# Recurrent mixer: the triangular solve's products cut to 32x32 blocks, and the solve's place in a slot made to alternate

## The reference, cut to what matters

```python
def wkv_scan(s0, scan_in):
    def step(s, inp):
        w, kk, a, k, v, r = inp
        sa = jnp.einsum('dbhij,dbhj->dbhi', s, kk)
        s = s * w[..., None, :] - sa[..., :, None] * (kk * a)[..., None, :] + v[..., :, None] * k[..., None, :]
        return s, jnp.einsum('dbhij,dbhj->dbhi', s, r)
    return lax.scan(step, s0, scan_in)
```

## Time and profile before

| what | value |
|---|---|
| median of 3 runs | 4435.7 us (4431.94 to 4444.57) |
| the profiled execution | 4427.04 us |
| its span, first to last instruction | 4425.4 us |
| granted TensorE clock, mean | 0.962 |
| iterations 0 to 16 of the mixer with its last products | about 706 us, from 2091 to 2797 us of the span |

### The profile page before, as it was taken

One profiled execution on the slowest core, in us unless ns is written; L12 is line 12 of the kernel. 1 busy time (PEld: TensorE's weight loads), 2 busy tenths in 40 slices (PEclk: granted clock), 3 DMA queues, 4 the chain that ended last, 5 costly groups with the idle time before them and its releaser, 6 DMA issues. The chain is left out here.

```text
span 4425.4 us, 76116 instructions
## 1 busy us (share of the span) xinstructions
PE 3997.9 (90%) x30302; PEld 2848.3 (64%) x30302; DVE 2760.9 (62%) x5967; ACT 1446.1 (33%) x3210; POOL 900.1 (20%) x926
## 2 busy tenths in 40 slices
PE   7989999998999899998999999898999777778777
PEld 6747887755788687787888888686444333333332
DVE  5674433665533566755666666245777888888885
ACT  3353342344523335712444444322111111111111
POOL 1101110110201101110000000101344444444443
PEclk9999999999999999999999999898999999999999
DMA  4203443311443310131000000434999999999998
GB/s 127 86 30 109 154 141 99 103 36 39 157 144 128 117 57 20 63 132 51 19 18 26 24 18 6 151 111 164 388 409 420 416 415 415 409 409 417 412 415 334
DMA packets 149522, 795.01 MB, mean 180 GB/s; under 512 B 18808, under 2 KB 22120, under 8 KB 82352
## 3 DMA queue, kind: packets, MB, share of 16 engines
q0 software_dynamic: 84560, 574.75, 32.2%
q1 hardware_dynamic: 57120, 188.06, 13.0%
q10 hardware_dynamic: 7488, 27.30, 1.9%
HBM read 765.84 MB, written 20.00 MB: 178 GB/s over the span
## 5 line engine op out<-in xcount | busy, mean ns | idle before, releaser
L3224 PE MATMUL psum<-rows,diag 128*128 128x512 f32 x2048 | 1007.3, 642 | 226.7 <-ACT diag L3103 207.7
L3224 PEld LDWEIGHTS psum<-rows,diag 128*128 128x128 f32 x2048 | 410.4, 205 | 779.5 <-issue 765.9
L2922 POOL DMA_INDIRECT rows<-in_peer_uv,sel_idx x512 | 612.6, 1197 | 739.7 <-PE psum L3224 675.4
L2965 DVE SCALAR_TENSOR_TENSOR uh<-rows,h_rows 128x1024 f32<-128x1024 f32 x512 | 628.1, 1227 | 208.1 <-DMA rows<-in_peer_uv,sel_idx 183.1
L529 DVE TENSOR_TENSOR w_split_lo<-w_raw,w_split_hi 128x1024 fp32r<-128x1024 f32 (+1 forms) x271 | 326.2, 1214 | 497.6 <-ACT w_split_hi L516 493.2
L516 ACT CAST w_split_hi<-w_raw 128x1024 fp32r<-128x1024 f32 (+1 forms) x271 | 276.4, 1027 | 621.4 <-PE psum L465 396.7
L3096 ACT ACTIVATE g<-g 128x4 f32<-128x4 f32 x128 | 26.3, 205 | 1092.5 <-DVE g L2976 1092.5
L693 POOL TENSOR_TENSOR uT_lo<-normed_rows,uT_hi 128x512 fp32r<-128x512 f32 x64 | 90.2, 1410 | 661.2 <-ACT uT_hi L669 661.2
L465 PE MATMUL psum<-hT_mlp_hi,w_split_hi 128*128 128x512 f32 x512 | 201.3, 393 | 5.5 <-DVE hT_mlp_lo L261 5.5
L465 PE MATMUL psum<-hT_mlp_lo,w_split_hi 128*128 128x512 f32 x512 | 200.2, 391 | 0.0
L465 PE MATMUL psum<-hT_mlp_hi,w_split_lo 128*128 128x512 f32 x512 | 200.2, 391 | 0.0
(11 more groups left out here) (523 smaller groups left out, 8465.6 us busy)
## 6 DMA issues: line engine op xcount, KB each, us to landing
w_raw<-in_w_in SPq DMA_DIRECT2D x105, 512.0 KB, 4.1
w_raw<-in_w_up SPq DMA_DIRECT2D x64, 512.0 KB, 4.5
w_raw<-in_w_down SPq DMA_DIRECT2D x64, 512.0 KB, 4.4
amask_sb<-in_w_mod ACTq DMA_DIRECT2D x48, 512.0 KB, 3.7
wq<-in_peer_wq SPq DMA_DIRECT2D x24, 512.0 KB, 7.9
rows<-in_peer_uv,sel_idx POOLq DMA_INDIRECT x512, 12.6
qkpad<-in_w_out SPq DMA_DIRECT2D x12, 512.0 KB, 5.5
w_raw<-in_w_out SPq DMA_DIRECT2D x12, 512.0 KB, 4.3
```

The costliest lines, as they stand in the source:

```text
L2922: nc.gpsimd.indirect_dma_start(out=rows[:, n % RB, :], out_offset=None, in_=I["peer_uv"], in_offset=bass.IndirectOffsetOnAxis(ap=sel[:, t, ...
L2965: nc.vector.scalar_tensor_tensor(prod[:], rows[:, n % RB, 0:D], 1.0, h[:, t, :], ALU.mult, ALU.mult, accum_out=dots[:, (n // BATCH) % 2, s ...
L3224: last = nc.tensor.matmul(psum[:, 2 * (t % 2) + half, :], diag[:, n % (2 * BATCH), :], rows[:, n % RB, D + half * NB:D + (half + 1) * NB], ...
```

## The change

Three things, in `rwkv_phase` only. Levels 1 to 4 of the solve use `by_quarter`: four products of 32x32 by 32x32 on the diagonal, in place of two of 64x64 by 64x64. Level 5 uses `across`: two 32x32 products, of the one block off the diagonal that is taken over. And on TensorE and ScalarE the order within a slot becomes solve, scan, fill, others in odd slots, and fill, others (with the scan ahead of them on ScalarE), scan, solve in even slots; on TensorE the Gram products of slots 0 to 2 move with the solve. VectorE's, GpSimd's and SyncE's queues stay as they are.

```diff
+    def by_quarter(out, lhsT, rhs):
+
+        for j, at in enumerate(quarters):
+            own = quarters[j % 2]
+            last = nc.tensor.matmul(out[at, own], lhsT[at, own], rhs[at, own], start=True, stop=True)
+        return last
+
+    def across(out, lhsT, rhs, source, target, mine, others):
+
+        for h in range(2):
+            rows = quarters[2 * h + source]
+            last = nc.tensor.matmul(out[quarters[2 * h + target], others], lhsT[rows, mine], rhs[rows, others],
+                                    start=True, stop=True)
         return last
...
-                        last = by_head(psum[:, b, i * L_CH:(i + 1) * L_CH], AT[:, c], X[:, c], True, True)
+                        out = psum[:, b, i * L_CH:(i + 1) * L_CH]
+                        if lv < LEVELS:
+                            last = by_quarter(out, AT[:, c], X[:, c])
+                        else:
+                            last = across(out, AT[:, c], X[:, c], d, 1 - d, quarters[1 - d], quarters[d])
...
-                        l_, r_ = (y, U[:, c]) if lv < LEVELS else (U[:, c], y)
-                        last = by_head(psum[:, b, i * L_CH:(i + 1) * L_CH], l_, r_, True, True)
+                        out = psum[:, b, i * L_CH:(i + 1) * L_CH]
+                        if lv < LEVELS:
+                            last = by_quarter(out, y, U[:, c])
+                        else:
+                            last = across(out, U[:, c], y, 1 - d, d, quarters[d], quarters[1 - d])
...
                 for k in range(SLOTS_):
-                    if build is not None:
+                    if build is not None and k % 2:
                         solve(k, build)
-                        if 3 <= k < 12:
-                            fill(k, build)
-                    if scanned is not None:
+                    if scanned is not None and k % 2:
                         scan(k, scanned)
+                    if build is not None and 3 <= k < 12:
+                        fill(k, build)
                     if prep and k in (0, 2, 4, 6):
                         lora_product(k, prep)
...
                         final_product(k, final, prep)
+                    if scanned is not None and k % 2 == 0:
+                        scan(k, scanned)
+                    if build is not None and k % 2 == 0:
+                        solve(k, build)
```

More of the change, by code:

```diff
@@ L1914, in rwkv_phase @@
     halves = (slice(0, 64), slice(64, P))
+    quarters = tuple(slice(32 * j, 32 * j + 32) for j in range(4))
     def cells(ap):
```

## The result

The changed kernel takes 4596.5 us (median of 4 runs, 4586.3 to 4612.2) against 4436.3 before: a ratio of 1.0362, with a 95% interval of 1.0327 to 1.0397. It is 160 us slower. The forecast was slower, by 38 us and at most 89. The profiled execution is the longest of the four; its span is 4610.5 us, 185 more than that of the kernel before.

A forecast was written before the change was run, and what follows sets the result against it. TensorE was taken to be full, its own issue order setting an iteration's length. Terms -6.4 + 4.3 + 1.25 + 2.9 = +2.05 us an iteration, x15 = +31, plus 7 for the clock, +38: 4474 us, range 4400 to 4525.

The forecast's parts named there:

- The step of small products: Solve on TensorE: four 32x32 products run together, a step takes 0.254 us instead of 0.467, saving 6.4 us an iteration.
- The neighbouring steps of scan and fill: TensorE waits for copies between steps now side by side: fill +2.9 us, scan +1.25 us an iteration.
- The changes of size: TensorE, between solve and other products: 0.27 us a pair of tile-size changes, 16 pairs, 4.3 us an iteration.
- the sum: All terms added: +2.05 us an iteration, +31 us over 15 iterations, with the clock +38 us.
- What moves for nothing: Operations queued behind VectorE's later solve copies in even slots, and loads on other queues: no cost.
- The clock: TensorE's granted clock falls after more holes: four more low stretches, 7 us, bounds 0 and 30.
- Rival 5: The clock stays low for long in the mixer, as small products leave array idle: +30 to +100 us, chance 0.05.
- rival 2: Solve products: fewer than four at a time, or a binding issue rate; two at a time gives 4566 us; chance 0.16.

The follow-up runs named there:

- r1: The kernel before with its 64x64 products, in the new order, with VectorE's queue put in that order as well: 4496.4 us, ratio 1.0139.
- e2: The kernel before with its 64x64 products kept, and only the new order on TensorE and ScalarE: 4538.2 us, ratio 1.0233.
- d1: The changed kernel with VectorE's queue turned as well, solve copy and turn last in even slots: 4559.3 us, ratio 1.0276.
- e1: The kernel before with the small 32x32 products, in the old order: 4520.6 us, ratio 1.0191.
- e3: e1 with half as many small products in levels 1 to 4, two in place of four a chunk: 4511.3 us, ratio 1.0161.
- w1: The changed kernel with unused 64x128 products put into four of TensorE's waits of an iteration: 4577.7 us, ratio 1.0332.
- e5: The kernel before, old order, with every 64x64 solve product made twice: 4631.1 us in one run.
- w2: d1 with unused products put into TensorE's remaining waits: 4559.3 us, ratio 1.0285.

## Why the prediction was wrong

The direction was right, and the size was not: 38 us forecast, 160 measured, outside the range.

**What held.** The step of small products: rounds of four come every 0.032 us, as forecast. The neighbouring steps of scan and fill: 2.9 + 1.25 us an iteration, x15 = 62 us, and the order with VectorE's queue turned as well (r1) costs 59. The changes of size are there, but a pair costs about 0.21 us and not 0.27, so that the 4.3 us an iteration were nearer 3.4. Had nothing else happened, the change would have cost (-6.4 + 3.4) x 15 + 59 = 14 us, half of the 31 that the sum has for it.

**"What moves for nothing" failed.** The prediction named the operations that queue behind VectorE's late copies and looked for who waits for them only in preparation, norms and finals. The fill's own reads in slot 6 stand there too, and TensorE's slot 7 waits for these: 24 waits for `gate_rows`, 25 us in sum. And `sq` did not keep its balance: the longest wait for it went from 1.6 to 2.7 us. r1 prices both at 44 us of e2's 103. In the changed kernel d1 gets 37 back. The term was put at nothing, and it could have been read from the queues.

**The clock was mis-sized.** The term was 7 us, with 30 as its upper bound, for holes in TensorE's work. The low clock lasts 212 us instead of 27, and e1 (144 us, few new waits for other engines) and e3 (263 us, TensorE in flight nearly all the time) show that small products bring it by themselves. Rival 5 had this mechanism with 30 to 100 us and a chance of 0.05, which was too little. What it cost of the 160 us is not settled. w1 shows 19 us for 116 us less of it, and that did not remove all; by the 0.32 of e3 the 185 us more would be about 60 us, an estimate.

**The fetch had no term.** Over the mixer matmuls wait 33 us without a releaser by the lines shown in the changed kernel, and 36 in e1, nearly all at multiples of 256 instructions. e3 (same tiles, half the rate) and e5 (more instructions, nearly the old rate) show that the rate makes them. The prediction weighed an issue rate that binds evenly (rival 2) and not a queue that runs empty.

**How the parts add up.** As an estimate: 14 us from the terms that were there, about 40 for VectorE's queue, about 35 of stops and about 60 of low clock make 149 of the 160. The parts act on each other: while TensorE waits for VectorE, instructions arrive and a low clock costs nothing. That reading fits w1 and w2, but it was not tested alone.

## What to carry to other kernels

Before an operation is moved on one queue, go through every other queue for what stands behind its consumer, also for parts of the same stage: the wait comes from the neighbour that was not moved. A smaller product can run as fast as hoped and still lose: look at how many instructions a microsecond it needs, and at the granted clock, with one run of the products alone. Compare iterations of the same kind: here those with final products and those with norm products differ by 0.3 us and more. And count what two changes share before their costs are added up. And waits that a trace shows at one place (here `sq`, 1.1 us, seven times) may be worth more than a new form for the main work: moving a consumer two slots gave 0.33% where the rewrite lost 3.6%.

## What the hardware showed unexpectedly

TensorE's granted clock was 0.73 over an iteration in which matmuls were in flight for 53.1 of 54.95 us, all solve products being 32x32 and only two tiles of them at a time (e3). It was 0.98 over the mixer with 64x64 products issued nearly without holes (e5). Its instructions come in packets of 16 KB, 256 of them in each. The supply kept up with 32 instructions in 0.47 us for 890 us on end but for five short stops, and not with 64 in 0.28 us: there TensorE stopped for 0.6 to 1.7 us, as a rule, at whole multiples of 256 instructions. And four 32x32 products on the diagonal of the array start within 0.02 us of each other, in f32, and the next four 0.03 us later.
